# The inner value strips of a linear recurrence by seven block products with stationary tokens

## What is computed

```python
def _hgrn_scan(q, k, v, logf, S):
    """S_t = diag(f_t) S_{t-1} + k_t v_t^T (k = 1 - f), o_t = S_t^T q_t."""
...
def _hgrn_branch(seg_c, seg_l, lb, gain, dtype):
...
    q, f, i, g = seg
    qh = hd(jax.nn.silu(q.astype(f32)))
    vh = hd(i)
    lf_f, k_f = _hgrn_gates(f[..., :H_K], lb[0])
    lf_b, k_b = _hgrn_gates(f[..., H_K:], lb[1])
...
    seg_c = _split_proj(xc @ w_in + b_in)
    seg_l = _split_proj(xl @ w_in + b_in)
```

## Time and profile before

| | us |
|---|---|
| median of three runs | 1975.35 |
| lowest, highest | 1972.21, 1975.98 |
| the profiled execution | 1971.99 |
| its span, first to last instruction | 1970.2 |
| three pairs of the recurrence, each | 61.2 |
| last pair, to the mean product | 51.4 |

### The profile page before, as it was taken

One profiled execution on the slowest core, in us unless ns is written; L12 is line 12 of the kernel. 1 busy time (PEld: TensorE's weight loads), 2 busy tenths in 40 slices (PEclk: granted clock), 3 DMA queues, 4 the chain that ended last, 5 costly groups with the idle time before them and its releaser, 6 DMA issues.

```text
span 1970.2 us, 31165 instructions
## 1 busy us (share of the span) xinstructions
PE 1945.2 (99%) x12449; PEld 1751.1 (89%) x12449; DVE 1241.7 (63%) x2513; ACT 565.9 (29%) x1363; POOL 218.7 (11%) x267
## 2 busy tenths in 40 slices
PE   9999999999999999999999999999999999999998
PEld 7878999977799998888888888888888989999998
DVE  5425897572378865899669565343456765766664
ACT  3343332224533313111110013322343323132212
POOL 6100430312014200000000001001212100000000
PEclk9999999999999999999999999999999999999999
DMA  6354555343545542555545364332222224545552
GB/s 199 112 187 137 165 165 161 111 151 114 172 150 171 182 140 79 182 166 164 166 152 173 116 190 136 119 90 86 86 65 67 83 67 148 172 134 167 171 177 81
DMA packets 272105, 273.60 MB, mean 139 GB/s; under 512 B 7982, under 2 KB 269338, under 8 KB 271962
## 3 DMA queue, kind: packets, MB, share of 16 engines
q1 hardware_dynamic: 270152, 267.65, 42.5%
q0 software_dynamic: 1216, 3.32, 0.6%
q10 hardware_dynamic: 594, 0.65, 0.1%
HBM read 270.38 MB, written 1.08 MB: 138 GB/s over the span
## 4 chain that ended last, share of the span: by engine, by line
PE 93%; DVE 4%; ACT 1%; issue 1%; DMA 1%; ACTq 0%; DVEq 0%; SPq 0%; PEldq 0%
PE bank L818 50%; PE bank L1324 10%; PE bank L796 8%; PE bank L1510 5%; PE bank L1559 2%; PE bank L966 2%; PE bank L1087 1%; PE bank L1610 1%; PE bank L1037 1%; PE bank L1494 1%; PE bank L1572 1%; PE bank L1046 1%; PE bank L1391 1%; PE bank L1235 1%; PE bank L1241 1%
## 5 line engine op out<-in xcount | busy, mean ns | idle before, releaser
L818 PE MATMUL bank<-arena,SQ 128*128 128x136 f32 (+2 forms) x2176 | 341.4, 308 | 0.1
L818 PEld LDWEIGHTS bank<-arena,SQ 128*128 128x128 f32 x2176 | 307.0, 191 | 17.2 <-ACT arena L1931 0.3
L818 PE MATMUL bank<-arena,W 128*128 128x136 f32 (+2 forms) x1824 | 272.6, 301 | 2.7 <-issue 2.1
L818 PEld LDWEIGHTS bank<-arena,W 128*128 128x128 f32 x1824 | 247.6, 191 | 15.4 <-issue 4.1
L1931 ACT ACTIVATE H<-bank 128x128 f32<-128x128 f32 (+1 forms) x260 | 82.3, 317 | 535.5 <-PE bank L818 535.5
L818 PE MATMUL bank<-U,W 128*128 128x136 f32 (+2 forms) x1296 | 194.6, 303 | 0.0
L818 PEld LDWEIGHTS bank<-U,W 128*128 128x128 f32 x1296 | 176.4, 191 | 11.0 <-issue 2.9
L796 PE MATMUL bank<-U,W 128*128 128x272 f32 (+1 forms) x576 | 133.1, 392 | 1.4 <-ACT U L2213 0.8
L3033 DVE SCALAR_TENSOR_TENSOR W<-W,CC 128x256 f32<-128x256 f32 x280 | 128.3, 483 | 7.0
L796 PEld LDWEIGHTS bank<-U,W 128*128 128x128 f32 x576 | 109.0, 190 | 24.6 <-issue 2.3
L818 PE MATMUL bank<-arena 128*128 128x136 f32 (+1 forms) x1024 | 124.1, 278 | 0.0
(11 more groups left out here) (459 smaller groups left out, 3117.9 us busy)
## 6 DMA issues: line engine op xcount, KB each, us to landing
W<-in_ffn_w_up_dram SPq DMA_DIRECT2D x44, 1024.0 KB, 5.1
W<-in_ffn_w_in_dram SPq DMA_DIRECT2D x44, 1024.0 KB, 5.1
W<-in_ada_w_dram SPq DMA_DIRECT2D x36, 1024.0 KB, 6.6
W<-in_mix_w_in_dram SPq DMA_DIRECT2D x36, 1024.0 KB, 5.3
W<-in_ffn_w_down_dram SPq DMA_DIRECT2D x16, 1408.0 KB, 6.6
W<-in_ffn_w_out_dram SPq DMA_DIRECT2D x16, 1408.0 KB, 6.3
W<-in_w_in_dram SPq DMA_DIRECT2D x21, 1024.0 KB, 5.3
W<-in_w_out_dram SPq DMA_DIRECT2D x8, 1024.0 KB, 8.5
```

The source lines that it names most:

```text
L818: last = mm(o, a(k), b[:, k], start=not adds and k == 0, stop=k == kt - 1, skip_group_check=True)
```

## The change

The inner value strip is now computed by seven block products, with the strip sums formed by GpSimd as for the forget strips and the same token sums `TBR`. The tokens stay the stationary operand: each of the seven products has four steps, and each step is two matmuls of 128 tokens by 128 columns. The strip has 28 steps in place of 32, and `ctx` in `WEAVE` goes from 12 to 8, so that forget strip 0 begins directly behind level 1, four steps earlier than before.

ScalarE gets four copies more in each pair (`kept_inner`), and its copies for forget strip 0 move: they stood behind `lookup` 2, 3, 4 and 5, and stand behind `lookup` 3, 4 and 5. VectorE gets `inner_late` after level 1 and `inner_rest` after level 2 in place of `inner` after levels 1 and 3. GpSimd forms three strips' sums in a pair instead of two, and adds the bias to the whole of `HI` (128 x 1024) in one operation. The snapshots `SNI` use two row slots of `W[2]` and `W[3]` that forget strip 1 uses too, so its first copy waits for `inner_rest`.

```diff
-WEAVE = dict(pre=14, diag=6, lev=(8, 8, 8, 8, 12, 8, 8, 8), ctx=12, av=4)
+WEAVE = dict(pre=14, diag=6, lev=(8, 8, 8, 8, 12, 8, 8, 8), ctx=8, av=4)
...
             def steps_i(r):
...
+                def add(b, c, tok, w, k, clear):
+                    for n in range(2):
+                        last = mm(bank[b][:, c + n * P:c + (n + 1) * P], tok[:, k, n * P:(n + 1) * P], w[:, k],
+                                  start=clear and k == n == 0, stop=k == 3, skip_group_check=True)
+                    return last
+
                 eng.wait_ge(S.land[r], p.next(S.land[r], 16))
-                for n, (b, c, tok) in enumerate([(2, 0, perm(0)), (2, SW, perm(P)), (3, 0, toks(2 * P)), (3, SW, toks(3 * P))]):
-                    if c == 0:
-                        take(b)
-                    for k in range(KD):
-                        last = mm(bank[b][:, c:c + SW], tok(k), W[r][:, k, :], start=k == 0, stop=k == KD - 1, skip_group_check=True)
...
+                take(2)
+                for k in range(4):
+                    ins = add(2, near, permuted_and_context(0, 0), raw(0, 0), k, True)
...
+                eng.wait_ge(S.wsum, p.next(S.wsum))
+                for k in range(4):
+                    ins = add(3, near, permuted_and_context(1, 1), WSR[3], k, False)
...
+                eng.wait_ge(S.wsum, p.next(S.wsum))
+                eng.wait_ge(S.snap, p.next(S.snap))
+                for k in range(4):
+                    ins = add(2, near, TBR[2], WSR[2], k, False)
...
+            def inner_bias(i):
+
+                eng.wait_ge(S.hi, p.next(S.hi))
+                bias = HIB[:, i * SW:(i + 1) * SW].unsqueeze(1).to_broadcast([P, 4, SW])
+                eng.tensor_tensor(HI[:, :, :], HI[:, :, :], bias, ALU.add).then_inc(S.hi, p.inc(S.hi))
+
+            strip_sums(0, True)
+            strip_sums(1)
+            eng.wait_ge(S.hib, p.next(S.hib, 16))
+            for i in range(PAIRS):
+                strip_sums(3)
+                if i + 1 < PAIRS:
+                    strip_sums(0)
+                inner_bias(i)
+                if i + 1 < PAIRS:
+                    strip_sums(1)
...
+            def kept_inner(which):
+
+                x, z, y = bank[2][:, 0:SEQ], bank[3][:, 0:SEQ], bank[3][:, SEQ:2 * SEQ]
+                for n in which:
+                    eng.wait_ge(S.prod, p.next(S.prod, 2 if n == 2 else 1))
+                    i, src = ((0, x), (3, z), (1, x), (2, y))[n]
+                    act(SNI[i], src, ACT.Copy).then_inc(S.snap, p.inc(S.snap))
...
+                kept_inner((0,))
                 lookup(i, 0)
+                kept_inner((1,))
...
                 for lev in range(2, 7):
                     eng.wait_ge(S.lev_full, p.next(S.lev_full))
                     lookup(i, lev)
-                    if more and lev == 2:
+                    if lev == 2:
+                        kept_inner((2, 3))
+                    if more and lev == 3:
                         kept(0, (0,))
-                    if more and lev == 3:
+                    if more and lev == 4:
                         kept(0, (1,))
-                    if more and lev == 4:
-                        kept(0, (2,))
                     if more and lev == 5:
-                        kept(0, (3,))
+                        kept(0, (2, 3))
+                    if lev == 6:
+                        eng.wait_ge(S.hi, p.next(S.hi))
+                        p.skip(S.hi)
+                    if more and lev == 6:
                         kept(1, (0,))
...
+            def inner_late():
+
+                eng.wait_ge(S.snap, p.next(S.snap, 4))
+                tt(HI[:, 2:4, 0:P], tiles_of(SNI[1]), tiles_of(bank[3][:, 0:SEQ]), ALU.add).then_inc(S.order_dve, p.inc(S.order_dve))
...
+            def inner_rest():
+
+                eng.wait_ge(S.prod, p.next(S.prod, 6))
+                tt(HI[:, 0:2, 0:P], tiles_of(SNI[0]), tiles_of(bank[2][:, SEQ:2 * SEQ]), ALU.add)
+                both = tiles_of(bank[2][:, 0:SEQ]).unsqueeze(1).to_broadcast([P, 2, 2, P])
...
                     if lev == 1:
-                        inner(i, 0)
-                    if lev == 3:
-                        inner(i, 1)
+                        inner_late()
+                    if lev == 2:
+                        inner_rest()
```

More of the change, by code:

```diff
@@ L1552, in steps_i @@
             def steps_i(r):
-                eng.wait_ge(S.land[r], p.next(S.land[r], 16))
-                for n, (b, c, tok) in enumerate([(2, 0, perm(0)), (2, SW, perm(P)), (3, 0, toks(2 * P)), (3, SW, toks(3 * P))]):
-                    if c == 0:
-                        take(b)
-                    for k in range(KD):
-                        last = mm(bank[b][:, c:c + SW], tok(k), W[r][:, k, :], start=k == 0, stop=k == KD - 1, skip_group_check=True)
-                        if c and k == KD - 1:
-                            sem = S.done[r] if b == 3 else S.half[r]
-                            last.then_inc(sem, p.inc(sem))
-                        yield
+                near, far = 0, SEQ
@@ new lines, in steps_i @@
+                take(2)
+                for k in range(4):
+                    ins = add(2, near, permuted_and_context(0, 0), raw(0, 0), k, True)
+                    if k == 3:
+                        ins.then_inc(S.prod, p.inc(S.prod))
+                    yield
+                take(3)
+                eng.wait_ge(S.wsum, p.next(S.wsum))
+                for k in range(4):
+                    ins = add(3, near, TBR[0], WSR[0], k, True)
+                    if k == 3:
+                        ins.then_inc(S.prod, p.inc(S.prod))
+                    yield
@@ new lines, in steps_i @@
+                eng.wait_ge(S.snap, p.next(S.snap))
+                for k in range(4):
+                    add(2, far, permuted_and_context(1, 0), raw(0, 1), k, False)
+                    yield
+                eng.wait_ge(S.snap, p.next(S.snap))
+                for k in range(4):
+                    ins = add(3, far, TBR[3], raw(1, 1), k, False)
+                    if k == 3:
+                        ins.then_inc(S.prod, p.inc(S.prod))
+                    yield
+                eng.wait_ge(S.wsum, p.next(S.wsum))
@@ new lines, in steps_i @@
+                for k in range(4):
+                    ins = add(2, near, TBR[1], WSR[1], k, False)
+                    if k == 3:
+                        ins.then_inc(S.prod, p.inc(S.prod))
+                    yield
+                eng.wait_ge(S.wsum, p.next(S.wsum))
+                for k in range(4):
+                    ins = add(3, near, permuted_and_context(1, 1), WSR[3], k, False)
+                    if k == 3:
+                        ins.then_inc(S.prod, p.inc(S.prod))
+                    yield
@@ L1565, in steps_g @@
+                eng.wait_ge(S.wsum, p.next(S.wsum))
+                eng.wait_ge(S.snap, p.next(S.snap))
+                for k in range(4):
+                    ins = add(2, near, TBR[2], WSR[2], k, False)
+                    if k == 0:
+                        ins.then_inc(S.done[r], p.inc(S.done[r]))
+                    if k == 3:
+                        ins.then_inc(S.prod, p.inc(S.prod))
+                    yield
+                p.skip(S.snap)
             def steps_g(r):
@@ L1857, in _, with strip_sums @@
             p.skip(S.wsum, wsum)
-            for n in range(2 * PAIRS):
-                r = n % 2
+            def strip_sums(r, first=False):
                 part = lambda t, h: W[r][:, 4 * h:4 * h + 4, t * P:(t + 1) * P]
@@ L3390, in pick, with tiles_of @@
                 eng.sem_inc(S.free[b], 1)
[L3392 to L3397 removed]
+            def tiles_of(v):
+                return v.rearrange("p (n m) -> p n m", n=2)
+            def inner_late():
+                eng.wait_ge(S.snap, p.next(S.snap, 4))
+                tt(HI[:, 2:4, 0:P], tiles_of(SNI[1]), tiles_of(bank[3][:, 0:SEQ]), ALU.add).then_inc(S.order_dve, p.inc(S.order_dve))
+                eng.wait_ge(S.order_dve, p.now(S.order_dve))
+                eng.sem_inc(S.free[3], 1)
+            def inner_rest():
+                eng.wait_ge(S.prod, p.next(S.prod, 6))
+                tt(HI[:, 0:2, 0:P], tiles_of(SNI[0]), tiles_of(bank[2][:, SEQ:2 * SEQ]), ALU.add)
+                both = tiles_of(bank[2][:, 0:SEQ]).unsqueeze(1).to_broadcast([P, 2, 2, P])
+                tt(HI[:, :, P:2 * P].rearrange("p (c n) m -> p c n m", c=2), SNI_LATE.rearrange("p c (n m) -> p c n m", n=2), both,
+                   ALU.add).then_inc(S.hi, p.inc(S.hi))
                 eng.wait_ge(S.hi, p.now(S.hi))
[L3399 removed]
+                p.skip(S.hi)
+                eng.sem_inc(S.free[2], 1)
             def carry(i, d):
@@ L3415, in _ @@
             p.meet("recurrence")
-            p.skip(S.wsum, 4 * 2 * PAIRS)
-            eng.wait_ge(S.hib, p.next(S.hib, 16))
+            p.skip(S.wsum, 4 * 3 * PAIRS)
             fold(0, 0)
```

14 lines of the change are left out of this document (7 added, 7 removed).

## The result

The changed kernel takes 2029.44 us (median of 4 runs, 2028.66 to 2032.07) against 1973.78 (1971.95 to 1975.98): a ratio of 1.0288, interval 1.0276 to 1.03. The forecast was 2021 with a range of 1996 to 2040, and slower with 0.90: right, with 8 us missing.

The account below looks back on a forecast made before the run. TensorE's own work was taken to bound the recurrence. Three pairs at +12.3 us (36.9), the last pair's 3.4 and the clock's 7.9 add 48.2 to 1971.99, giving 2020.2, stated as 2021 with a range of 1996 to 2040.

Parts of the forecast that it names:

- What bounds the kernel: Recurrence: TensorE's own work sets the end; a microsecond of matmul removed is gained, and any wait is paid in full.
- The matmuls: Inner value strip: 28 steps of two 128-column matmuls replace 32 of one 256-column matmul, gaining 1.3 us a pair.
- The first stall: After level 0, TensorE waits for the third inner snapshot behind the level-2 key copy: 4.9 us, 3.9 without collision.
- The second stall: After level 2, TensorE waits for strip 0's second snapshot behind the level-4 key copy: 8.3 us, 5.0 without collisions.
- held once, for a while: Second stall: lower price of the bias operation's hold on VectorE, 1.0 us, making the forecast about 5 us lower.
- to its end: Second stall: upper price, VectorE held until GpSimd's bias operation is over, 2.3 us; the one taken.
- The rest of a pair: Strip 0's first and third snapshots cost 0 to 1.2 us, taken as 0.4; other copies and the bias are hidden.
- The last pair: Six steps a level: stalls of 1.6 us after level 0 and some 2.7 at level 4; +3.4 us in all.
- The clock: Lower TensorE clock after the second stall costs 2.6 us a pair, 7.9 in all; nothing after the first.
- No collisions: Rival: stalls in the recurrence without GpSimd collisions or clock loss, 7.6 us a pair, 1996 us; chance 0.18 (1995 to 2008).
- The clock down until the next wait: Rival: TensorE stays at the lower clock after both stalls, up to 14 us more a pair, 2033 to 2054; chance 0.17.
- The gain: Rival: the snapshots arrive in time and only the matmuls count, 1967 us, or 1970 as a median; chance 0.08.

Follow-up runs that it names:

- the filled stalls: Changed kernel with useless matmuls in TensorE's two stalls: 20 before the third inner snapshot (6 in the last pair), 34 before strip 0's second: 2017.08 us, ratio 1.0228.
- the version of 1979.49 us: Changed kernel with bank copies, including strip 1's first two, moved ahead of key copies and the bias behind strip 1's sums (last pair: after its last level): 1979.49 us, ratio 1.0033.

## Why the prediction was right, and where its 8 us went

*What bounds the kernel.* Right: TensorE was busy for the whole of each pair, and every wait on it was paid in full, and more than in full.

*The matmuls.* Right: 48 records of 128 columns from 1484.77 to 1490.13 are 0.1117 us each, against 0.1116 forecast (the rows that it names, 1.78 us for 16, give 0.1113; the gain is 1.3 us either way). The 1.3 us of a pair are there, but about 0.7 a pair is lost again at seams, breaks in the stream of records, that the sum didn't price: each stall also costs some 0.16 us of overlap between records (a group of 16 lasts 1.95 us but is followed by the next after 1.79), and in the second and third pair the diagonal product begins 1.09 us after the eight records ahead of it, which take 0.89 at full pitch.

*The first stall.* Forecast 4.9, measured 5.07, 5.06 and 5.50. The order rows gave its place and the rows of ScalarE its size. The collision is there too: a sum at 1498.32 beside the second scan, which takes 1.68 instead of 0.69:

```profile
1498.32 1.43 POOL L1916 TENSOR_TENSOR W<-W 128x512 f32<-128x512 f32 x1 [1.84 <-PE bank L1564]
1498.61 1.68 DVE L3502 TENSOR_TENSOR_SCAN arena<-arena,ones_row 128x255 f32<-128x255 f32 x1
```

*The second stall.* Forecast 8.3, measured 8.14, 8.14 and 7.99. Of its terms the bias (2.3) was measured at 2.14 by leaving it out. The Trainium skill, "SBUF — State Buffer", section "SBUF: two separate sides", had spoken for the upper end; the trace agrees, 2.34 us of GpSimd holding the scans for 2.14. The choice between "held once, for a while" at 1.0 and "to its end" at 2.3 was one between 2016 and 2021, and the second was right.

*The rest of a pair.* Forecast 0.4, measured 0.38, 0.39 and 0. No transfer and no copy besides came late.

*The last pair.* Forecast +3.4 with stalls of 1.6 and 2.7; measured 1.77 and 2.59, and 54.35 us from its first matmul to the merge where it was 51.23 (1586.59 to 1637.82): +3.1. The wait at the start of the merge grew from 1.05 to 1.68 us; the forecast had 0.4 for it, inside the last pair's 3.4.

*The clock.* This is the term that was mis-sized. The forecast took 2.6 us a pair, all after the second stall, and "nothing after the first". Both stalls pay. The slow records less their normal time come to 2.8 us after the first (3.75 for 1.95, 1.91 for 1.12, 3.81 for 3.62) and 1.5 after the second, 2.5 and 3.1 in the third pair: 14.2 us by the rows of three pairs, 12.8 in those pairs by the filled stalls. The step that failed is the reading of the earlier trace rows: there 2.7 us of idleness had been enough for the lower clock, and a first stall forecast at 4.9 us is longer; the sum put nothing behind it all the same, without a reason. The bound from both sides, 0 to 7 us after either stall, held: measured 2.5 to 2.8 and 1.5 to 3.1.

Put together, three pairs of 13.6 (stalls) + 4.7 (clock, from 14.2 over three) + 0.7 (seams) - 1.3 are 53.1 us; measured 53.0. The last pair's 3.1 and the 0.6 of the merge's wait make it 56.8 of the 56.7 found. Against the forecast's 48.2 the missing 8.5 are 6.3 of clock, 2.0 of seams and 0.6 at the merge, less 0.3 in the last pair, to rounding. The 2021 also adds 0.8 of the 3.4 us between the profiled run and the median, and nothing says why that much; 3.4 us is also the difference between the two ways in which the kernel starts. So the pair windows are 78 to 80 us and not the 73 to 77 that were to show it.

*The rivals.* No collisions (1996) is excluded by the scans of 4.45 us. The clock down until the next wait (2033 to 2054) is excluded too: the records were back at full pace 3 to 6 us after each stall, before the next one. The gain (1967 to 1970) would have needed copies that don't stand behind key copies. Even with that done, and the bias moved and the weave shifted, 1975.26 is what was reached. Whether another order of strips reaches it wasn't tried.

## What to carry to other kernels

A copy in an in-order queue is as late as the operation ahead of it. Before a copy is put behind another engine's result, ask when that result comes and who waits for the copy; here moving copies ahead in one queue gave back 33 of 56 us, and the saved matmuls are worth 5. On a TensorE that is busy all the time, price a wait with the slow records behind it as well: waits of 2.08 to 2.12 us cost 1.7 us more in six of seven cases here, and nothing in the seventh. Work given to an idle GpSimd isn't free when VectorE, which it holds up, is on the way to TensorE, and every wait that is taken away lets such work pile up elsewhere, so the next wait is read from the new trace, not from the old one.

## What the runs showed of the hardware

The granted clock after waits of TensorE in the recurrence and at the start of the merge, in all versions. After waits of 1.28 to 1.84 us the records behind were at full pace in every case (1.96 to 2.02 us for a group of 1.89 to 1.95). Between 2.0 and 3.1 us it went both ways, even in one kernel at one place: 2.41 us twice left eight records at 1.99 us, and 2.40 in the next pair left them at 3.50. Waits of 3.03 to 3.05 us cost nothing once, 1.7 us twice and 3.0 once. After 3.27 us and more the records behind were slow each time, and the cost didn't grow with the wait: 1.5 us behind 8.14, 3.1 behind 7.99, 2.8 behind 5.06, and 1.6 behind the same 5.06 in the version with strip 0's copies ahead. How the chip decides on it the runs don't show.

An elementwise GpSimd operation of 128x1024 takes 2.34 us and holds VectorE's scans for 2.14 of them. VectorE operations that read a bank weren't held in the cases seen: in the version of 1979.49 us the additions L3417 and L3418 take 0.42 and 0.68 us beside a sum, as they do alone. Three sums back to back stretched what ran beside them from 0.69 to 1.57 and from 0.28 to 1.35 us.

This kernel starts in one of two ways, 3.4 us apart. In the nine traces in which TensorE waits 0.57 to 1.34 us for one small transfer the granted clock is 1.00 from 10 to 23 us, in the four with 1.57 to 2.22 us it is 0.74; that the transfer is the cause wasn't tested; with effects of a few microseconds in question, spans are better compared from a common point inside the kernel.
